# Five edits at the end of a decoder step with 16 experts: tile 0's picks, the root table, tile 2's rows, the sample rows and tile 3's h rows

## What is computed

```
h = layer_norm(ALPHA * x + m, ln1_g, ln1_b)
# moe_ffn: router picks the best group of experts, two experts of it, gates sum to 1
for e in range(N_EXPERTS):
    u = silu(t @ w_gate[e]) * (t @ w_up[e])
    out = out + gates[:, e:e + 1] * (u @ w_down[e])
y = layer_norm(ALPHA * h + f, ln2_g, ln2_b)
```

## Time and profile before

| | |
|---|---|
| median of 3 runs | 1024.87 us (1024.86 to 1025.07) |
| the profiled execution | 1024.97 us |
| its span, first to last instruction | 1023.1 us |
| mean granted TensorE clock | 0.992 |
| PE / DVE / ACT / POOL busy | 98% / 78% / 47% / 37% of the span |
| chain that ended last | PE 91%, DVE 4%, the rest 5% |

### The profile page before, as it was taken

The page is one execution under the profiler, slowest core; times in us unless marked ns, Lnnn a source line. Parts: engine busy times, 40 slices in busy tenths (PEclk is TensorE's granted clock), DMA queues, the critical chain, the costliest instruction groups (busy, mean ns, idle before and its releaser), DMA issues.

```text
span 1023.1 us, 19648 instructions
## 1 busy us (share of the span) xinstructions
PE 998.7 (98%) x7238; PEld 903.7 (88%) x7238; DVE 793.0 (78%) x981; ACT 477.4 (47%) x675; POOL 373.6 (37%) x288
## 2 busy tenths in 40 slices
PE   8999999999999999999999999997999999999996
PEld 7999999999999999999999999985677777777773
DVE  4698889888989996753444498237989899898997
ACT  4232322223232335234443233342878787888875
POOL 3344444444455655344544444420200000000264
PEclk9999999999999999999999999998999999999998
DMA  7432323323232222333224531737999999999854
GB/s 221 121 103 83 101 84 95 90 84 100 82 103 82 83 83 72 100 103 102 82 83 157 191 103 56 294 115 281 399 387 400 388 397 389 399 395 377 318 173 177
DMA packets 147290, 190.55 MB, mean 186 GB/s; under 512 B 6819, under 2 KB 114339, under 8 KB 147228
## 3 DMA queue, kind: packets, MB, share of 16 engines
q1 hardware_dynamic: 140107, 176.74, 49.7%
q0 software_dynamic: 3008, 10.55, 3.3%
q10 hardware_dynamic: 4129, 2.67, 1.0%
HBM read 179.16 MB, written 11.76 MB: 187 GB/s over the span
## 4 chain that ended last, share of the span: by engine, by line
PE 91%; DVE 4%; issue 2%; DMA 2%; ACT 1%; POOL 0%; ACTq 0%; SPq 0%; DVEq 0%; POOLq 0%
PE pr L1131 60%; PE pr L1324 16%; PE work L1324 8%; DMA sb_tok<-in_state_conv_b_dram 1%; PE work L1300 1%; PE work L1213 1%; PE work L1357 1%; PE pr L1365 1%; ACT ring L904 0%; DMA hs<-h_rows,ids 0%; PE work L1238 0%; PE work L1139 0%; PE work L1439 0%; PE pr L1289 0%; DVE w_down_lo L1776 0%
## 5 line engine op out<-in xcount | busy, mean ns | idle before, releaser
L608 POOL TENSOR_TENSOR w_lo<-raw,w_hi 128x512 fp32r<-128x512 f32 x208 | 296.9, 1447 | 326.5 <-ACT w_hi L760 326.5
L1131 PE MATMUL pr<-x_hi,w_hi 128*128 128x260 f32 x1264 | 255.2, 283 | 0.0
L1131 PE MATMUL pr<-x_hi,w_lo 128*128 128x260 f32 x1264 | 254.7, 283 | 0.0
L1131 PE MATMUL pr<-x_lo,w_hi 128*128 128x260 f32 x1264 | 254.3, 283 | 0.0
L764 ACT ACTIVATE ev<-pr 128x520 f32<-128x520 f32 x96 | 58.1, 605 | 372.9 <-PE pr L1131 372.9
L1131 PEld LDWEIGHTS pr<-x_hi,w_hi 128*128 128x128 f32 x1264 | 195.0, 188 | 0.3
L1131 PEld LDWEIGHTS pr<-x_hi,w_lo 128*128 128x128 f32 x1264 | 194.9, 188 | 0.0
L1131 PEld LDWEIGHTS pr<-x_lo,w_hi 128*128 128x128 f32 x1264 | 194.3, 188 | 0.0
L1593 DVE SCALAR_TENSOR_TENSOR work<-b_pad,par,work 128x512 f32<-128x512 f32 x224 | 148.1, 742 | 0.0
L760 ACT ACTIVATE w_hi<-raw 128x512 fp32r<-128x512 f32 x208 | 118.9, 623 | 2.8 <-DMA raw<-in_w_in_dram 2.3
L645 POOL DMA_INDIRECT hs<-h_rows,ids x15 | 19.3, 1287 | 247.4 <-DVE ids L1887 247.4
(11 more groups left out here) (408 smaller groups left out, 1737.5 us busy)
## 6 DMA issues: line engine op xcount, KB each, us to landing
raw<-in_w_in_dram SPq DMA_DIRECT2D x80, 512.0 KB, 3.7
w_gate<-in_expert_w_gate_dram SPq DMA_DIRECT2D x16, 2048.0 KB, 14.6
w_up<-in_expert_w_up_dram SPq DMA_DIRECT2D x16, 2048.0 KB, 13.5
w_down<-in_expert_w_down_dram SPq DMA_DIRECT2D x16, 2048.0 KB, 12.6
y_rows<-y_out SPq DMA_DIRECT2D x14, 384.0 KB, 12.3
raw<-in_w_a_out_dram SPq DMA_DIRECT2D x8, 512.0 KB, 3.9
raw<-in_w_c_out_dram SPq DMA_DIRECT2D x8, 512.0 KB, 4.0
raw<-in_w_b_out_dram SPq DMA_DIRECT2D x8, 512.0 KB, 4.1
```

What stands on the lines that cost most here:

```text
L608: pool.tensor_tensor(w_lo[:, slot, k], raw[:, slot, k], w_hi[:, slot, k].bitcast(F32), ALU.subtract).then_inc(w_split, 1)
L1131: mm = pe.matmul(pr[slot][:, h, 0:HALF], w[:, slot, k, :], x[:, k, h * HALF:(h + 1) * HALF], start=(k == 0 and w is w_hi and x is hi), sto ...
```

## The change

In VectorE's last expert, `partial(0)` goes ahead of the last expert's down low parts, `partial(1)` and `partial(2)` each move up one place, and `others_first` goes ahead of the two `share_low`. In the tail VectorE makes the samples' sum ahead of tile 3's sum, closes the upper 512 columns of tile 2 itself, and finishes the samples ahead of tile 3's normalising. ScalarE follows: it copies the samples before tile 2's deviation, takes the samples' mean and squares before tile 3's deviation, scales only half of tile 2, and makes the 1x1 root (with its table load) before the last expert's rows instead of at the start of `finish`. GpSimd adds the bias to half of tile 2. SyncE sends five pieces instead of four. TensorE adds tile 3's h rows in four pieces of 256 columns, with a straight read and an output of stride two.

```diff
@@ results_out (SyncE)
-                for b in range(3):
-                    sp.wait_ge(added, b + 1)
-                    sp.dma_start(y_prompt[0, b * P:(b + 1) * P, :], y_b[:, b, :]).then_inc(fin_out[0], 16)
-                sp.wait_ge(fin_ready, 3)
+                def rows_to(b, cols):
+                    sp.dma_start(y_prompt[0, b * P:(b + 1) * P, cols], y_b[:, b, cols]).then_inc(fin_out[0], 16)
+
+                sp.wait_ge(added, 1)
+                rows_to(0, slice(0, D))
+                sp.wait_ge(fin_ready, 1)
+                rows_to(2, slice(D // 2, D))
+                sp.wait_ge(added, 2)
+                rows_to(1, slice(0, D))
+                sp.wait_ge(fin_ready, 2)
                 sp.dma_start(y_sample[:, 0, :].rearrange("s (c f) -> (s c) f", f=CS), sy_a).then_inc(fin_out[0], 16)
+                sp.wait_ge(added, 3)
+                rows_to(2, slice(0, D // 2))
@@ add_rows (GpSimd), and the same cut in scaled (ScalarE)
-                    pool.tensor_tensor(y_b[:, b, :], y_a[:, b, :], ln2_rows[:, 1, :], ALU.add).then_inc(added, 1)
+                    cols = slice(0, D // 2 if b == 2 else D)
+                    pool.tensor_tensor(y_b[:, b, cols], y_a[:, b, cols], ln2_rows[:, 1, cols], ALU.add).then_inc(added, 1)
@@ last_rows_out (ScalarE)
                     act.activation(y_a[:, 3, :], y_a[:, 3, :], ACT.Copy, scale=s_wa[:, 3:4]).then_inc(end_act, 1)
+                    act.activation(r_tok[0:1, 0:1], eps_t[0:1, 0:1], ACT.Sqrt)
                     for h in range(2):
@@ normalised (ScalarE)
                 scaled(0)
-                deviation(2)
                 act.wait_ge(var_ready, NORMED[0])
                 act.activation(sz_in, sy_a, ACT.Copy).then_inc(end_act, 1)
+                deviation(2)
                 scaled(1)
-                deviation(3)
-                scaled(2)
                 act.wait_ge(end_mm, 7)
                 act.activation(s_agg[:, 1:2], pr[0][:, 0, 2 * CS:2 * CS + 1], ACT.Copy, scale=-1.0).then_inc(end_act, 1)
                 act.wait_ge(end_act, 6)
                 act.activation(sy_b, sz, ACT.Square, bias=s_agg[:, 1:2], accum_out=s_agg[:, 2:3]).then_inc(end_act, 1)
+                deviation(3)
                 act.wait_ge(end_mm, 8)
                 act.activation(s_agg[:, 3:4], pr[0][:, 0, 2 * CS + 2:2 * CS + 3], ACT.Sqrt, bias=eps_t[:, 1:2]).then_inc(end_act, 1)
+                scaled(2)
                 for h in range(2):
-                    act.wait_ge(fin_ready, 1 + h)
+                    act.wait_ge(fin_ready, 3 + h)
...
             def finish():
-                act.activation(r_tok[0:1, 0:1], eps_t[0:1, 0:1], ACT.Sqrt)
                 normalised()
@@ share_last (TensorE)
-                by_pair = h_back[:, 3, :].rearrange("p (i g) -> p g i", i=2)
                 for h in range(2):
-                    pe.matmul(z_tile[3][:, h, :].rearrange("p (g i) -> p g i", i=2), ident[:], by_pair[:, h * D // 4:(h + 1) * D // 4, :], start=True, stop=False)
+                    for i in range(2):
+                        cols = slice(i * D // 2 + h * D // 4, i * D // 2 + (h + 1) * D // 4)
+                        pe.matmul(z_tile[3][:, h, :].rearrange("p (g i) -> p i g", i=2)[:, i, :], ident[:], h_back[:, 3, cols], start=i == 0, stop=False)
@@ expert_pass (VectorE)
                         if ps is first:
                             share_marks()
+                            dve.wait_ge(back_in, 48)
+                            partial(0, 16)
...
                 if ps is first:
-                    dve.wait_ge(back_in, 48)
-                    partial(0, 16)
+                    partial(1, 16)
...
                 if ps is first:
-                    partial(1, 16)
+                    partial(2, 16)
                     spread_samples()
-                    partial(2, 16)
+                    others_first()
                     share_low(0)
                     share_low(1)
-                    others_first()
@@ results (VectorE)
                 normalise(1)
-                summed_up(3)
-                normalise(2)
...
                 do(dve.scalar_tensor_tensor(sz, sy_b, s_spread[:, 4:5], sz_in, ALU.mult, ALU.add, accum_out=s_agg[:, 0:1]), Tally(dve, end_dve, 4))
                 last[0] = chain
-                normalise(3)
+                summed_up(3)
+                normalise(2)
+                settle()
+                upper = slice(D // 2, D)
+                do(dve.scalar_tensor_tensor(y_b[:, 2, upper], y_a[:, 2, upper], agg[:, 2, 3:4], ln2_rows[:, 1, upper], ALU.mult, ALU.add), to_fin)
...
                 do(dve.scalar_tensor_tensor(sy_a, sz, s_agg[:, 3:4], sln2[:, 1, :], ALU.mult, ALU.add), to_fin)
+                last[0] = chain
+                normalise(3)
```

More of the change, by code:

```diff
@@ L584, in _ @@
             results_out()
-            sp.wait_ge(fin_out[0], 64)
+            sp.wait_ge(fin_out[0], 80)
             sp.wait_ge(fin_out[1], 32)
@@ L1037, in scaled @@
                 act.wait_ge(var_ready, NORMED[b])
-                act.activation(y_a[:, b, :], y_a[:, b, :], ACT.Copy, scale=agg[:, b, 3:4]).then_inc(std2_ready, 1)
+                cols = slice(0, D // 2 if b == 2 else D)
+                act.activation(y_a[:, b, cols], y_a[:, b, cols], ACT.Copy, scale=agg[:, b, 3:4]).then_inc(std2_ready, 1)
             def normalised():
```

## The result

The changed kernel takes 1030.18 us, median of 4 runs (1029.37 to 1032.3), against 1024.86 before on the same chip: a ratio of 1.0055 (taken over the single runs; the quotient of the two medians is 1.0052), with 1.0039 to 1.0071 as the 95% interval. It is slower by 5.3 us, where 0.6 less was forecast. The profiled execution took 1029.47, 1.8 more than its span.

The account below looks back on a forecast made before the run. TensorE until 1011.96, then VectorE and the last transfer were taken as the bound. With a 0.5 us slip, 0.43 saved and the tail's new order, the landing came at 1022.1 against 1022.8: 1024.97 - 0.65 = 1024.3 us, range 1023.2 to 1025.9.

Parts of the forecast that it names:

- What bounds it: Chain ending last: TensorE without a gap until 1011.96, then VectorE, then SyncE's sample rows, landing at 1022.8.
- VectorE isn't late for it: At tile 3's sum, forecast to start at 1012.1: VectorE would be free at 1011.9.
- Part 1: Tile 0's picks moved on VectorE: GpSimd is held, the gathered rows land at 1000.6, tile 0's own rows 0.5 us later.
- The six operations that ran in and behind the hole fall as follows: GpSimd's index operations, held by VectorE, end at 990.8, 992.0, right behind, 993.5, 994.7 and 994.9 instead of 992.0.
- 0.5 us later: Tile 0's own rows on TensorE end at 1004.1, and everything behind them on TensorE moves by 0.5.
- point of decision: Sign of the slower case at the gather: tile 0's rows landing behind 1003.1.
- second rival: GpSimd's first gather is held longer: 1025.4 for one missed gap (chance 0.2), 1026.9 for two (chance 0.05).
- Part 2: Root table load of 1.28 us on ScalarE moves behind the scaling of tile 3, fits but for 0.1; gain taken: nothing.
- Part 3: Tile 3's h rows on TensorE in eight half passes: 1.72 us instead of 2.16, 0.43 us saved.
- third rival: Strided output of the h rows costs a full pass per piece: +1.72, 1026.0, with the gather's miss 1027.1; chance 0.08.
- Part 4: Order of the tail: tile 3's sum to its normalising takes 4.6 us instead of 3.19; landing at 1022.1 against 1022.8.
- its last half is now the last transfer: Tile 3's last half, issued at 1019.7, lands in 2.3 us plus 0.1 for SyncE's queue, at 1022.1.

Follow-up runs that it names:

- the first experiment: The whole change, but with VectorE's last expert in the order of before (picks and `others_first` in their old places): 1024.78 us, ratio 0.9994 to the kernel before.
- the last experiment: As the first experiment, but SyncE sends tile 1's rows ahead of tile 2's upper half: 1024.71 us, ratio 0.9996 to the kernel before.
- the idle operation: Kernel before plus one VectorE operation in the hole, like `partial`, two inputs in SBUF, result unused: 1030.29 us, ratio 1.0042.

## Why the prediction was wrong, step by step

**What bounds it: right before the change, off by 0.1 us in it.** TensorE to tile 3's own rows, then VectorE; with the h rows cut in pieces VectorE is the last, by 0.1 us ("VectorE isn't late for it" had 0.2 to spare the other way). I missed that TensorE's passage rested on GpSimd with 2.3 us to spare: the spread product ran at 994.29, the cast ended at 992.01. It had no idle time then, so no row of waits named it; the code does (`pe.wait_ge(const_ready, 7)` ahead of `down_last`).

**Part 1: wrong, in two steps, and here the forecast failed.** "The six operations that ran in and behind the hole fall as follows", with the cast ending at 994.9: the first two fell as I wrote (990.97 and 992.17 for 990.8 and 992.0), the third should have come "right behind" and ended at 994.88, the fourth at 997.68 instead of 993.5, and the cast at 998.07, 3.2 us beyond the forecast. The prediction let each operation wait for one of VectorE's at most. The second step is one that it lacks: TensorE's wait for the cast, and the lower clock behind it, stand in none of its terms. Even with a cast at 994.9 TensorE would have waited, 0.6 us. "0.5 us later" for tile 0's own rows became 5.0: TensorE's first product on a tile starts at 1005.81, where it was 1000.76 in the kernel before. The working: the spread product comes 3.8 us later (998.12 for 994.29), the passes behind it take 1.6 us more by the lower clock, and 0.3 of waiting that stood there before is gone. Of these 5.0 us the h rows' pieces give 0.4 back ahead of tile 3's sum, which makes the 4.6 of the profile.

**The point of decision of the second rival** ("a landing of tile 0's rows behind 1003.1") asked for a longer hold, but at another place, and looked at one of three consumers. It let GpSimd's gather be held behind a cast at 994.9; the gather of 998.86 took 1.10 us, and the operations ahead of the cast were held. That the rows landed near its 1003.2 is luck. They did land at 1003.5 (`others_first` started at 1003.48), just behind it, but by then TensorE was 5 us late, and `share_low` waited for TensorE's product, not for the gather. Its price, 1026.9 at a chance of 0.05, was 3.3 us short.

**Part 2: right.** The table load runs at 1002.18 for 1.28 us, unseen.

**Part 3: right.** TensorE's timeline after:

```profile
1012.02 1.89 PE L1476 MATMUL work<-h_back,ident 128*128 128x256 f32 x8
1013.75 1.88 PE L1449 MATMUL work<-y_a,ident 128*128 128x512 f32 x4
```

Eight passes in 1.73 us (1012.02 to 1013.75), 0.216 each, where the earlier trace rows have 2.16: 0.43 saved, and the third rival, with the rule of the Trainium skill on non-contiguous patterns in PSUM behind it ("SBUF — State Buffer", Door 1), is not borne out for an output of stride two.

**Part 4: its work near, its end wrong.** Tile 3's sum to its normalising took 4.3 to 4.45 us (forecast 4.6), the wait for GpSimd's addition included (the upper half took 0.90 in the first experiment, 0.76 after). The branch of TensorE stayed unseen: the samples' mean came at 1016.68, right behind their sum. But "its last half is now the last transfer" isn't what ends the program. It lands in 3.2 us, not in 2.3 + 0.1, and with the 2.3 of the last experiment the end stays where it was, since ScalarE's closing comes 3.4 us or more behind its last issue. A term for that is missing: with it the new order is worth 0.2 us by the spans, not 0.65. The first experiment (1024.78, where the kernel before took 1025.18) may show a gain and can't prove one.

## What to carry to other kernels

Before an idle stretch of VectorE is filled with an operation that reads two operands from SBUF, see what GpSimd does in it: it may be the only time in which GpSimd gets through, and one operation of 1.2 us put its last result off by 6 us here. Then list everything that waits for GpSimd's result, from the code's waits and not from the profile's, since a wait that is met in time shows in no row; here there were three such paths, and taking away one or two of them gave nothing back, in part because an engine that no longer waits runs into GpSimd's work at another place. And when TensorE is made to wait some microseconds, price the passes behind it at the lower clock.

## What the runs showed of the hardware

- The hold is not one operation long. A GpSimd operation that began behind the start of a two-input VectorE operation was let through at its end (1.12 us at 989.85 and 1.24 at 990.93 above, likewise 1.12 and 1.11 with the idle operation). One that had begun ahead of such an operation, by 0.08 to 0.52 us, was held through it and the next: 2.61 and 2.74 us above, 2.53 and 2.91 with the idle operation, though it takes 0.17 to 0.25 in the kernel before. Where no second one stood behind, it was held through one: the COPY of 1.50 us, 0.2 us ahead of a `partial`. The Trainium skill ("SBUF — State Buffer", Who interferes with whom) says that the second to start waits for the whole of the first; the measured holds here are up to twice that, and those that suffer had started first by the profile. Why is open, also why the 0.52 us, with VectorE's operations on PSUM, weren't enough for the last of them.
- The granted clock didn't fall with the idle time but behind it: the first passes still started 0.23 us apart, those from 999.81 on 0.42 to 0.43, and from 1003.03 on 0.23 again. In this case 3.6 us of idle time cost 1.6 us more behind it.
- A program's end can lie on an engine that has only issued a transfer: ScalarE's closing `DRAIN` came 3.41 us behind its last issue where that piece landed after 2.3 us, and 3.54 where it landed after 3.2.
